# Token-by-token projections of a two-block kernel: products with 512 moving columns in place of 256, two buffers placed anew, state products per head

## What is computed

```python
for l in range(2):
    h = _rms(x, norm_g[l])
    proj = h @ w_in[l]
    (gq, gk, gv, ga, gz, bq, bk, bv, iq, ik, iw, bz,
     cq, ck, cv, cz, gate) = jnp.split(proj, SPLIT_AT, axis=-1)
    y_a = _gla(gq, gk, gv, ga, ...) * jax.nn.silu(gz)      # gated linear attention, chunks of 64
    y_b = _dsa(bq, bk, bv, iq, ik, iw, ...) * jax.nn.silu(bz)  # top-k attention, 4 heads of 128
    y_c = _diff(cq, ck, cv, ...) * jax.nn.silu(cz)         # differential attention, 4 heads
    g = jax.nn.sigmoid(gate)
    merged = g_a * (y_a @ w_br[l, 0]) + g_b * (y_b @ w_br[l, 1]) + g_c * (y_c @ w_br[l, 2])
    x = x + merged @ w_out[l]
# _gla, per head (4 heads, 64 keys, 128 values) and chunk c of 64 tokens:
#   u_c = k_dec_c.T @ v_c;  S_c = decay_c * S_{c-1} + u_c;  o_c = q_c @ S_c
```

## Time and profile before

| | |
|---|---|
| median of 3 runs | 2025.89 us (2024.94 to 2026.28) |
| the profiled execution | 2027.14 us, of it the span 2025.3 us |
| granted TensorE clock | 0.996 of full speed |
| PE, PEld busy | 98%, 84% of the span |
| DVE, ACT, POOL busy | 59%, 45%, 17% |
| DMA | 88 GB/s over the span |

### The profile page before, as it was taken

The page is one execution under the profiler, slowest core; times in us unless marked ns, Lnnn a source line. Parts: engine busy times, 40 slices in busy tenths (PEclk is TensorE's granted clock), DMA queues, the critical chain, the costliest instruction groups (busy, mean ns, idle before and its releaser), DMA issues.

```text
span 2025.3 us, 28962 instructions
## 1 busy us (share of the span) xinstructions
PE 1994.7 (98%) x11531; PEld 1692.1 (84%) x11531; DVE 1185.5 (59%) x1869; ACT 913.0 (45%) x1486; POOL 353.7 (17%) x190
## 2 busy tenths in 40 slices
PE   7999999999999999999999999999999999999999
PEld 6977777788787877998998798887898998798887
DVE  6776555476453556687545645455589545655443
ACT  5454456443333345433445454344543444545332
POOL 1020002212020121244020100231235110010211
PEclk9999999999999999999999999999999999999999
DMA  5221111332222223223121123223222222122221
GB/s 209 79 87 42 43 63 68 120 105 98 89 104 83 104 105 123 84 84 104 53 92 66 45 87 122 84 83 145 80 79 93 66 81 84 47 82 84 105 104 63
DMA packets 25460, 179.08 MB, mean 88 GB/s; under 512 B 2944, under 2 KB 3584, under 8 KB 4864
## 3 DMA queue, kind: packets, MB, share of 16 engines
q1 hardware_dynamic: 23616, 164.24, 23.2%
q10 hardware_dynamic: 1728, 13.24, 1.7%
HBM read 171.18 MB, written 6.29 MB: 88 GB/s over the span
## 4 chain that ended last, share of the span: by engine, by line
PE 91%; ACT 3%; DVE 3%; DMA 1%; DVEq 0%; issue 0%; POOL 0%; SPq 0%; ACTq 0%
PE pp L258 27%; PE pp L260 26%; PE pp L259 26%; ACT whi L247 1%; DVE wlo L252 1%; PE po L260 1%; PE po L259 1%; PE po L258 1%; PE ps L659 1%; PE pt L934 1%; PE ps L1009 1%; PE ps L960 1%; PE pt L706 1%; PE po L910 1%; PE pt L1217 1%; DMA wraw<-weights 1%
## 5 line engine op out<-in xcount | busy, mean ns | idle before, releaser
L258 PE MATMUL pp<-hhi,whi 128*128 128x512 f32 (+2 forms) x1096 | 443.1, 404 | 7.3 <-DVE wlo L252 3.8
L260 PE MATMUL pp<-hhi,wlo 128*128 128x512 f32 (+2 forms) x1096 | 430.7, 393 | 0.0
L259 PE MATMUL pp<-hlo,whi 128*128 128x512 f32 (+2 forms) x1096 | 430.3, 393 | 0.0
L252 DVE TENSOR_TENSOR wlo<-wraw,whi 128x2048 fp32r<-128x2048 f32 x125 | 289.7, 2318 | 226.3 <-ACT whi L247 225.2
L258 PE MATMUL pp<-whi,hhi 128*128 128x256 f32 x1344 | 393.0, 292 | 0.3
L259 PE MATMUL pp<-wlo,hhi 128*128 128x256 f32 x1344 | 380.1, 283 | 0.0
L260 PE MATMUL pp<-whi,hlo 128*128 128x256 f32 x1344 | 379.9, 283 | 0.0
L247 ACT ACTIVATE whi<-wraw 128x2048 fp32r<-128x2048 f32 x151 | 287.8, 1906 | 2.6 <-DMA wraw<-weights 2.6
L258 PEld LDWEIGHTS pp<-whi,hhi 128*128 128x128 f32 x1344 | 257.4, 192 | 13.2 <-issue 7.2
L259 PEld LDWEIGHTS pp<-wlo,hhi 128*128 128x128 f32 x1344 | 257.4, 191 | 0.5
L260 PEld LDWEIGHTS pp<-whi,hlo 128*128 128x128 f32 x1344 | 257.2, 191 | 0.0
(11 more groups left out here) (367 smaller groups left out, 2526.3 us busy)
## 6 DMA issues: line engine op xcount, KB each, us to landing
wraw<-weights SPq DMA_DIRECT2D x152, 1024.0 KB, 4.8
out_t<-xT ACTq DMA_DIRECT2D x4, 1024.0 KB, 3.9
xT<-out_t ACTq DMA_DIRECT2D x2, 2048.0 KB, 8.7
xT<-x_t SPq DMA_DIRECT2D x4, 512.0 KB, 7.1
work<-cmp_w ACTq DMA_DIRECT2D x1, 2048.0 KB, 7.3
xT<-x_t ACTq DMA_DIRECT2D x1, 2048.0 KB, 8.1
out_t<-xT SPq DMA_DIRECT2D x4, 512.0 KB, 2.6
work<-small ACTq DMA_DIRECT2D x3, 128.0 KB, 3.3
```

The source lines that it names most:

```text
L252: nc.vector.tensor_tensor(wlo[:, slot, :], wraw[:, slot, :], whi[:, slot, :].bitcast(F32), ALU.subtract).then_inc(w_lo, 1)
L258: nc.tensor.matmul(out_ap, ah, bh, start=start, stop=False)
L259: nc.tensor.matmul(out_ap, ah, bl, start=False, stop=False)
L260: return nc.tensor.matmul(out_ap, al, bh, start=False, stop=stop)
```

## The change

**Chunks.** The 19 sections take chunks of half the rows: 512 rows (4 row blocks) of all 512 columns. A section still has two chunks of 1 MB, but only four tiles, of 128 tokens x 512 columns, and every tile needs both chunks. A matmul has 512 moving columns.

**Open tiles.** A tile is made in two passes of 4 row blocks x 3 = 12 matmuls, one pass per chunk; between them it stays open in its bank. `pe_wide` numbers the passes p = 0 to 7. For `q bq bk bv cz` all four tiles are open at once (banks `po[0]`, `po[1]`, `pp`), in the order `IN_FOUR`: tiles 0 to 3 with the first chunk, then 0 to 3 with the second. For `cq ck cv gv gz` two are, in the order `IN_TWO`: tiles 0, 1 with the first chunk, 0, 1 with the second, then 2, 3 and 2, 3. The first chunk's slot is then free after p = 3 or after p = 5, the second's after p = 7. ACT's conversions follow the new semaphore `a_free` and the last tile (`act_after_first`, `act_after_second`). ACT copies out 512 columns at once (`act_wide`), four times per section in place of eight.

**State products per head.** For each 128-token block there are now 8 matmuls, one per head and chunk, of 64 rows x 64 stationary x 128 moving columns, issued at even c for two chunks together; `st_f` has 128 columns per head pair in place of 256.

**Buffers.** `split` and `work` are allocated ahead of the small tensors. In the built program they now start at multiples of 128 bytes; before, 64 bytes past one.

**Moves.** The transposes after `cz` go to `ps` in place of `po`. On DVE two weight conversions of the DSA attention move from step i = 1 to i = 2 (s = 1 and 3), and one from c = 4 to c = 6 in the linear attention.

```diff
-BLOCK2 = [("ikg", 1, 1), ("iq", 2, 2), ("bq", 2, 4), ("bk", 2, 4), ("bv", 2, 4), ("bgate", 4, 2), ("bz", 2, 2),
+BLOCK2 = [("ikg", 1, 1), ("iq", 2, 2), ("bq", 2, 2), ("bk", 2, 2), ("bv", 2, 2), ("bgate", 4, 2), ("bz", 2, 2),
...
+WIDE = ("bq", "bk", "bv", "cq", "ck", "cv", "cz", "gv", "gz")
+FOUR_BANKS = ("q", "bq", "bk", "bv", "cz")
+IN_FOUR = [(i, half) for half in range(2) for i in range(QT)]
+IN_TWO = [(2 * pair + i, half) for pair in range(2) for half in range(2) for i in range(2)]
...
+        split = sb("split", [P, 11328], F32R)
+        work = sb("work", [P, 15360], F32)
         vec, cst, msk = sb("vec", [P, NVEC], F32), sb("cst", [P, NCST], F32), sb("msk", [P, NMSK], BF16)
...
-        work = sb("work", [P, 15360], F32)
-        split = sb("split", [P, 11328], F32R)
...
+        def wide_bank(name, l, i):
+            par0, _ = par_of(name, l)
+            return po[i] if name in FOUR_BANKS and i < 2 else pp[(par0 + i) % 2]
+
+        def pe_wide(pe, name, l, p, first=0, end=4, ready=None):
+            c0, _, t0, _ = section(name, l)
+            _, slot0 = par_of(name, l)
+            four = name in FOUR_BANKS
+            i, half = (IN_FOUR if four else IN_TWO)[p]
+            if first == 0:
+                if i == 0:
+                    pe.wait_ge(w_lo, c0 + half + 1)
+                if half == 0:
+                    pe.wait_ge(evac, t0 + i - (3 if four else 1))
+            wh, wl = weights((slot0 + half) % 2, 4, 512)
+            tt = slice(i * P, i * P + P)
+            for x in range(first, end):
+                k = 4 * half + x
+                if ready is not None:
+                    ready(k)
+                last = three(wide_bank(name, l, i)[:, :], (hhi[:, k, tt], hlo[:, k, tt]), (wh[:, x, :], wl[:, x, :]),
+                             k == 0, k == KT - 1)
+            if end == 4 and half == 1:
+                last.then_inc(mm_done, 1)
+            if end == 4 and half == 0 and i == QT - 1:
+                last.then_inc(a_free, 1)
...
+        def act_after_first(act, name, l):
+            act.wait_ge(a_free, 1 if l is None else 2 + len(WIDE) * l + WIDE.index(name))
+            act_next(act, name, l, section(name, l)[0], par_of(name, l)[1])
...
@@ pe_layer, DSA attention, step (s, i) @@
-                    pe_tm_tile(pe, ("cq", "ck", "cv")[s // 2], l, 4 * (s % 2) + i, 0, 4)
+                    pe_wide(pe, ("cq", "ck", "cv")[s // 2], l, 4 * (s % 2) + i, 0, 2)
...
-                    pe_tm_tile(pe, ("cq", "ck", "cv")[s // 2], l, 4 * (s % 2) + i, 4, 8)
+                    pe_wide(pe, ("cq", "ck", "cv")[s // 2], l, 4 * (s % 2) + i, 2, 4)
...
@@ pe_layer, linear attention @@
-                    for hp in range(2):
-                        last = nc.tensor.matmul(pt[c % 2][:, 256 * hp:256 * hp + 256], kd_f[rows, i, hp * P:hp * P + P],
-                                                gv_f[rows, i, 256 * hp:256 * hp + 256], start=True, stop=True)
-                    last.then_inc(u_done, 1)
-                    pe_tm_tile(pe, "gz", l, c)
+                    i = c // 2
+                    if c % 2 == 0:
+                        if c >= 2:
+                            pe.wait_ge(state_ready, 8 * l + c)
+                        for hd in range(4):
+                            for b in range(2):
+                                rows = y_rows(b)
+                                last = nc.tensor.matmul(pt[b][y_rows(hd % 2), P * (hd // 2):P * (hd // 2) + P],
+                                                        kd_f[rows, i, 64 * hd:64 * hd + 64],
+                                                        gv_f[rows, i, P * hd:P * hd + P], start=True, stop=True)
+                                if hd == 3:
+                                    last.then_inc(u_done, 1)
+                    pe_wide(pe, "gz", l, c)
...
@@ act_layer, DSA attention, step (s, i) @@
+                    if p == 5:
+                        act_after_first(act, name, l)
+                    if p == 7:
+                        act_after_second(act, name, l)
...
@@ dve_layer, DSA attention, step (s, i) @@
-                    if s >= 1 and i == 1:
+                    if s in (1, 3) and i == 2 or s in (2, 4) and i == 1:
                         if s == 1:
                             dve.wait_ge(w_lo, c0 + 2)
                         dve_conv(dve, c0 + s + 1, (slot0 + s - 1) % 2)
...
@@ _stream @@
+    def rows(m):
+        put(m[0:512])
+        put(m[512:1024])
...
-        columns(w[:, 4184:4696])
+        rows(w[:, 4184:4696])
```

More of the change, by code:

```diff
@@ L596, in two_block_kernel @@
         gv_f, gk_f = wv(10240, 4, S), wv(13824, 4, 256)
-        st_f = [wv(12288 + 512 * b, 2, 256) for b in range(2)]
+        st_f = [wv(12288 + 512 * b, 2, P) for b in range(2)]
         dec_f, wa2_f = wv(14848, 2, 8), wv(12288, 256)
@@ L1095, in pe_layer @@
                 pe_dots(pe, l, p)
[L1096 to L1099, removed]
+            for p in range(4, 8):
+                pe_wide(pe, "bk", l, p)
+            for p in range(8):
+                pe_wide(pe, "bv", l, p)
             pe_fm(pe, "bgate", l, h, KT, 256)
@@ L1181, in pe_layer @@
             pe_pv_tm(pe, v0 + 3, 3, vr[1], po[1])
-            for n in range(4):
-                pe_tm_tile(pe, "gv", l, n)
+            for p in range(4):
+                pe_wide(pe, "gv", l, p)
             pe.wait_ge(wa2_in, 16 * (l + 1))
@@ L1189, in pe_layer @@
             last.then_inc(z_done, 1)
-            for n in range(4, 6):
-                pe_tm_tile(pe, "gv", l, n)
+            for p in range(4, 6):
+                pe_wide(pe, "gv", l, p)
             for x in range(4):
@@ L1194, in pe_layer @@
                 pe_t(pe, D_BANKS[x], o_tm[:, x, :])
-            for n in range(6, 8):
-                pe_tm_tile(pe, "gv", l, n)
+            for p in range(6, 8):
+                pe_wide(pe, "gv", l, p)
             pe_fm(pe, "gq", l, h, KT, 256)
@@ L1403, in act_layer @@
             for c in range(8 + 1):
-                if c < 8:
-                    act_tm_tile(act, "gz", l, c, by_token(z_a, c), ACT.Silu)
+                t, half = IN_TWO[c] if c < 8 else (0, 0)
+                if half == 1:
+                    act_wide(act, "gz", l, t, z_a[:, t, :], ACT.Silu)
                 if c == 1:
@@ L1769, in _ @@
             pe.wait_ge(lam_in, 1)
-            nc.tensor.matmul(po[0][:, 0:4], ones, lam[:, 0:4], start=True, stop=True).then_inc(lam_sum, 1)
+            nc.tensor.matmul(pt[1][:, 0:4], ones, lam[:, 0:4], start=True, stop=True).then_inc(lam_sum, 1)
             for j in range(4):
@@ L1773, in _ @@
             pe_fm(pe, "cmp", None, h, KT, 256, h_ready(pe, 0))
-            pe_tm(pe, "q", None, 256)
+            for p in range(8):
+                pe_wide(pe, "q", None, p)
             pe.wait_ge(cmp_in, 32)
@@ L1926, in _ @@
             act.wait_ge(lam_sum, 1)
[L1927 to L1936 removed]
+            nc.scalar.activation(lam[:, 4:8], pt[1][:, 0:4], ACT.Exp).then_inc(lam_exp, 1)
+            act_after_first(act, "q", None)
+            for i in range(QT):
+                act_wide(act, "q", None, i, q_tm[:, i, :])
+            act_after_second(act, "q", None)
             act.drain()
@@ L2471, in _stream @@
     q = w[:, 512:1024].reshape(D, 2, 4, 64).transpose(0, 2, 1, 3).reshape(D, 512)
-    columns(q)
+    rows(q)
     put(kv[:, [2, 4]].reshape(D, 256))
```

166 lines of the change are left out of this document (83 added, 83 removed).

## The result

The changed kernel takes **1995.7 us** (median of 4 runs, 1992.9 to 1996.8) against 2025.8 us before: 0.985 of it, 95% interval 0.9833 to 0.9867, so 27 to 34 us less. The forecast of 1995 us and its range of 1985 to 2008 held. The span of the profiled execution went from 2025.3 to 1995.0 us.

What follows compares the result with a forecast made beforehand. PE, busy 98% of the span and holding 91% of the chain of waits, bounds the kernel. Terms -19.8 - 7.3 - 12.7 + 8.4 + 0.6 = -30.8 us against the 2025.9 us median give 1995 us, range 1985 to 2008.

Steps and rivals of the forecast that it cites:

- A: Weight sections: 3648 matmuls of 256 columns become 1824 of 512, and wider products save 19.8 us.
- D: DSA attention: PE waits about 2 us for second weight chunks at (2, 2) and (4, 2), both layers; +8.4 us.
- E: Small waits of PE before the linear attention and for `cq`'s second chunk at (0, 2); +0.6 us.
- Rival 4: Weight sections: width saves little, only the low end of the wider products' gain; 2003 us, chance 0.04.
- B: Linear attention's state products: row halves overlap, 1.0 us per block, saving 0.91 us for each of 8 blocks; -7.3 us.
- rival 3: Linear attention: state products fold fourfold, overlapping by rows and columns, for -11.1 us; 1991 us, chance 0.13.
- C: Products moving from `split`: starting on a multiple of 128 bytes quickens 1872 matmuls by 0.0065 us each; -12.7 us with scores.
- Rival 1: Products moving from `split`: its placement is worth nothing; 2008 us, chance 0.17.
- Rival 2: DSA attention: the four long waits don't come because DVE gets ahead; 1987 us, chance 0.05.
- costed at nothing: Slot refills, the top-k chain's third pass and ACT's copies of 512 columns: no time lost.
- rival 5: Ten sections with two open tiles: each of 20 slot refills 2.6 us late, 52 us; 2039 us, chance 0.02.

Runs made afterwards that it cites:

- mended kernel: The changed kernel with DVE's low-part conversion of `ck`'s and `cv`'s second chunks issued earlier in steps (2, 1) and (4, 1): 1984.9 us, 0.9794 of before.

## Why the prediction was right, and where not

The sum was -30.8 us, and the measurement -30.0 (27 to 34). The total is better than its parts: two terms were wrong in opposite directions, and a third was right in size for a false reason. By its steps:

- **A, wider products, -19.8: confirmed.** Twelve passes of `bk` and `bv` won 1.90 us, forecast 12 x 0.158 = 1.90. Twelve passes between dots won 1.39, forecast 1.56. The run with width and its waits alone gave -11.1 where A, D and E said -10.8. Rival 4 falls. The Trainium skill's formula for an isolated product (TensorE: Matmul & The Clock Gate, Back-to-back issue gap) gives 0.216 us for 512 columns; these rows have 0.2267, and by them the width was worth 11 us with its waits and about 21 without, not 4.6.
- **B, state products, -7.3: mis-sized.** The term took overlap by row halves alone, since no row showed more. The columns overlap as well, as rival 3 said, 0.60 us a block for 1.0. Rival 3's -11.1 (by its own 0.5 us a block it is 8 x 1.41 = 11.3) was too much, by the block's 0.60 and by the output products, slower by 0.1 us each in six of eight places of a layer, a price that neither named. The run with this part alone shows 5.11 us a layer, **-10.2** in both by its trace, and -11.3 (8.7 to 14.2) by its times.
- **C, placement, -12.7: the size right, its cause wrong.** -12.8 in the run with 64 bytes of padding, and 65.28 us for 288 products where 0.0065 x 288 off 67.20 gives 65.33. But the step said "now `split` starts on a multiple" of 128, and that is not what counts: with `hhi` and `split` on such a multiple and the weights on another the gain was gone. The size was read from two paces; that the new start would give the quicker one was luck. It does because it agrees with `whi`'s modulo 256, which the old one didn't. Rival 1 falls. The Trainium skill names 16-byte cachelines (SBUF — State Buffer, the table of specifications); they do not explain it, since all places tried are multiples of 16.
- **D, new waits, +8.4: the waits right, in place and in size; a cost behind them left out.** Two a layer, at (2, 2) and (4, 2), for the reason given, 7.4 us in the list of waits and 8.5 us of the stage's time (94.95 against 90.7 in each layer). Rival 2 falls. What the term put at nothing, without naming it, is the clock behind them: 1.6 us at each fall, none to two falls in an execution. The mended kernel gave 10 us back.
- **E, +0.6: hardly seen.** L1248 (L1201 before) starts 0.33 us after the product ahead of it, where it was 0.23, so 0.1 us a layer for the 0.2 forecast; its weight load waits for DVE (0.7 us in both layers). `cq`'s chunk is in no list of waits. What was costed at nothing stayed so: there is no wait for `wlo` or `whi` in `cz`, `gv` or `gz`, and rival 5 has nothing for it.

The kernels of the parts gave -11.1 for width with its waits, -11.3 for the state products (-10.2 by the trace) and -12.8 for the placement: -34 to -35. The 4 to 5 us to the measured -30 lie within the intervals of the three runs together (2.7 us each), so the parts are not known better than that. What can be said is that B was too small by about 3 us and D by about 2, in opposite directions, and that the close total owes something to that.

## What to carry to other kernels

When a tile is split so that it needs its second chunk sooner, look in the trace for the engine that makes that chunk, and move its work into the idle time just ahead, before making the change; here DVE had 2.08 us of idle just ahead, and two moved lines were worth 10 us, a third of the whole. Before placing large operands, read the pace of long stretches by moving and stationary buffer: 3% of their pace hung on the starts agreeing modulo 256 bytes. A gain that comes as forecast doesn't prove its reason: only a run that broke the rule (`split` 64 bytes off a multiple of 128 and at 0.2290 in place of 0.2333) showed that mine was wrong.

## What the runs showed of the hardware that was not expected

- The pace of an fp32r product of 128 x 128 with 512 moving columns depends on the difference of the two operands' starts modulo 256 bytes: 0.2267 us at 0, 0.2290 at 64, 0.232 to 0.233 at 32, 96, 128, 192 and 224. Shifting `hhi`, `hlo` and `split` by 128 bytes against the weights cost about 30 us in 1995, by one run.
- fp32 products on 64 x 64 quarters of the array overlap by rows and by columns, in either order of issue: sixteen records of 128 columns in 0.60 us.
- An output product whose successor has another stationary shape takes 0.1 us longer (0.65 against 0.55 us for the same eight records).
- An idle stretch of 2.0 us of PE, at (4, 2), was followed by a granted clock of 0.57 to 0.62 over some 4 us in 14 of 20 places, for 1.6 us each; one of 1.7 us at (2, 2) never was. Around the idle stretch of 1.6 us at the start of a layer the clock fell to 0.50 to 0.58, and for longer in some executions than in others, which moves the time of an execution by a microsecond or two.
